# Matmuls by segment, modulation units summed by DVE and a float32r ones matmul, and Q's raw slabs in h's context columns, in a two-layer GLA and attention trunk

## The reference

```python
mod_x = jnp.einsum('bd,lde->lbe', jax.nn.silu(c), w_ada) + b_ada[:, None, :]
mod_c = jnp.einsum('d,lde->le', jax.nn.silu(c_ctx), w_ada) + b_ada
for i in range(DEPTH):                       # DEPTH = 2
    sh1, sc1, g1, sh2, sc2, g2 = jnp.split(mod_x[i][:, None, :], 6, axis=-1)
    ...                                      # the same of mod_c for the context
    hx = rmsnorm(x, norm_mix[i]) * (1.0 + sc1) + sh1
    hc = rmsnorm(ctx, norm_mix[i]) * (1.0 + csc1) + csh1
    ...                                      # layer 0: gated linear attention (GLA), both directions
    ...                                      # layer 1: windowed attention with sinks; q, k rotated (RoPE)
    x = x + g1 * ox
    x = x + g2 * swiglu(rmsnorm(x, norm_ffn[i]) * (1.0 + sc2) + sh2, ffn_w_in[i], ffn_w_out[i])
    if not last:                             # the context goes through layer 0 alone
        ctx = ctx + cg1 * oc
        ctx = ctx + cg2 * swiglu(...)
return rmsnorm(x, norm_final)
```

## Time and profile before

| | us |
|---|---|
| median of 3 runs | 1669.13 |
| the profiled execution, its own time | 1669.12 |
| its span from first to last instruction | 1667.4 |
| PE busy in the span | 1618.1 |
| DVE busy in the span | 864.4 |
| ACT busy in the span | 577.4 |
| mean granted clock of TensorE, as a share | 0.989 |

### The profile page before, as it was taken

One profiled execution on the slowest core, in us unless ns is written; L12 is line 12 of the kernel. 1 busy time (PEld: TensorE's weight loads), 2 busy tenths in 40 slices (PEclk: granted clock), 3 DMA queues, 4 the chain that ended last, 5 costly groups with the idle time before them and its releaser, 6 DMA issues.

```text
span 1667.4 us, 24130 instructions
## 1 busy us (share of the span) xinstructions
PE 1618.1 (97%) x9568; PEld 1370.2 (82%) x9568; DVE 864.4 (52%) x1426; ACT 577.4 (35%) x833; POOL 99.2 (6%) x96
## 2 busy tenths in 40 slices
PE   7999999999999999999999999979999999999998
PEld 5889988888888888888888888757778788888886
DVE  5314436644576566556566336678755533333334
ACT  4315447542432111122102124457744422222223
POOL 0000000000000000000000000036540000000003
PEclk8999999999999999999999999979999999999999
DMA  9341310013443433343343213320003232333332
GB/s 335 100 128 54 106 44 26 26 51 102 127 127 101 125 127 112 115 126 102 125 126 103 74 57 108 101 76 2 1 1 101 76 101 87 90 100 101 101 88 88
DMA packets 197310, 156.07 MB, mean 94 GB/s; under 512 B 6691, under 2 KB 194255, under 8 KB 197231
## 3 DMA queue, kind: packets, MB, share of 16 engines
q1 hardware_dynamic: 197230, 154.97, 30.4%
HBM read 149.71 MB, written 2.10 MB: 91 GB/s over the span
## 4 chain that ended last, share of the span: by engine, by line
PE 88%; DVE 4%; ACT 4%; issue 1%; SPq 1%; DMA 1%; DVEq 0%; ACTq 0%
PE ps L577 85%; PE ps L1110 1%; ACT w_hi L1189 1%; DVE w_lo L1667 1%; DMA ada_pre<-in_w_ada 1%; PE ps L1115 1%; SPq L376 1%; DVE q_st L2192 1%; DVE h_lo L1730 1%; DVE scaled L1721 0%; ACT h_hi L1239 0%; ACT pr L1624 0%; DMA q_sw<-q_rot 0%; PE ps L892 0%; SPq L495 0%
## 5 line engine op out<-in xcount | busy, mean ns | idle before, releaser
L577 PE MATMUL ps<-h_hi,w_hi 128*128 128x256 f32 (+1 forms) x1392 | 422.3, 362 | 6.9 <-DVE w_lo L1667 6.8
L577 PE MATMUL ps<-h_hi,w_lo 128*128 128x256 f32 (+1 forms) x1392 | 413.6, 355 | 0.0
L577 PE MATMUL ps<-h_lo,w_hi 128*128 128x256 f32 (+1 forms) x1392 | 410.1, 353 | 0.0
L1667 DVE TENSOR_TENSOR w_lo<-w_raw,w_hi 128x2048 fp32r<-128x2048 f32 (+1 forms) x88 | 197.2, 2240 | 219.1 <-ACT w_hi L1189 218.9
L577 PEld LDWEIGHTS ps<-h_hi,w_hi 128*128 128x128 f32 x1392 | 257.3, 190 | 51.9 <-issue 13.5
L1189 ACT ACTIVATE w_hi<-w_raw 128x2048 fp32r<-128x2048 f32 (+1 forms) x88 | 165.1, 1876 | 386.0 <-DMA w_raw<-in_ffn_w_in 207.3
L577 PEld LDWEIGHTS ps<-h_lo,w_hi 128*128 128x128 f32 x1392 | 263.7, 189 | 38.3
L577 PEld LDWEIGHTS ps<-h_hi,w_lo 128*128 128x128 f32 x1392 | 262.9, 189 | 37.0
L577 PE MATMUL ps<-a_hi,w_hi 128*128 128x512 f32 (+1 forms) x528 | 160.5, 359 | 0.0
L577 PE MATMUL ps<-a_hi,w_lo 128*128 128x512 f32 (+1 forms) x528 | 160.1, 358 | 0.0
L577 PE MATMUL ps<-a_lo,w_hi 128*128 128x512 f32 (+1 forms) x528 | 158.0, 354 | 0.0
(11 more groups left out here) (246 smaller groups left out, 2011.7 us busy)
## 6 DMA issues: line engine op xcount, KB each, us to landing
w_raw<-in_ffn_w_in SPq DMA_DIRECT2D x88, 512.0 KB, 4.9
ada_w<-in_w_ada SPq DMA_DIRECT2D x41, 1024.0 KB, 5.3
w_raw<-in_ffn_w_out SPq DMA_DIRECT2D x32, 512.0 KB, 4.4
w_raw<-in_gla_w_in SPq DMA_DIRECT2D x24, 512.0 KB, 4.9
ada_pre<-in_w_ada SPq DMA_DIRECT2D x7, 1024.0 KB, 11.8
w_raw<-in_ffn_w_out SPq DMA_DIRECT2D x16, 384.0 KB, 3.5
w_raw<-in_gla_w_o SPq DMA_DIRECT2D x8, 512.0 KB, 7.2
w_raw<-in_swa_w_o SPq DMA_DIRECT2D x8, 512.0 KB, 5.0
```

What stands on the lines that cost most here:

```text
L577: return pe.matmul(o, w, r, start=start, stop=stop, skip_group_check=skip)
L1667: dve.tensor_tensor(w_lo[s][:, 0:kc, :], raw_of(n)[:, 0:kc, :], w_hi[s][:, 0:kc, :].bitcast(F32), ALU.subtract).then_inc(wlo_ok, 1)
```

## The change

1. **Order within a chunk.** Wherever PE works on both segments, the loops become segment (LAT first), ch, product: six matmuls of 512 columns, then six of 256.
2. **Units 0 to 3 and 12 to 39** go by DVE's `unit_acc`. ACT makes a float32r copy of the result (`unit_high`), DVE the rest (`unit_low`), and PE sums both with two float32r matmuls of 512 columns against a matrix of ones, which leaves the sums in all partitions of bank 7. DVE picks the diagonal: a product with `ident`, a reduction, and the bias (`store_sum`). Units 4 to 11 stay with `unit`. There are two sets of `u_acc`, `u_hi`, `u_lo` and ones, one for units 0 to 3 and one for the rest.
3. **Places.** In the GLA's Q and K the sums stand ahead of chunks 1 and 7 of slab 2 and chunk 6 of slab 3; unit 3's in V0 at tile 2, where the first gate pre-activation moves to tile 3. FFN0's first two slabs have no unit any more, and all others up to slab 45 have one (28 in all). SP asks for unit 1 ahead of slab 3.
4. **Q's stage.** Raw slabs Q0 + 2 and Q0 + 3 land in the context columns of `h_hi` and `h_lo` (`raw_c`), free once the KV slab is done. SP asks for them before the first swap. ACT splits Q0 + 1 between chunks 4 and 5 of h, and Q0 + 2 ahead of `raw_q(0)`; DVE's split of Q0 + 2 comes before K's low part. `q_rot` sets rotate over four, `v_tok` is copied by ACT, and `high(5)` comes before `raw_q(6)`.

The core of the diff:

```diff
-                    for ch in chunks:
-                        blk = slice(ch * P, (ch + 1) * P)
-                        for j, (w, r) in enumerate(((w_hi, x_hi), (w_hi, x_lo), (w_lo, x_hi))):
-                            for sg in segs:
+                    for sg in reversed(segs):
+                        for ch in chunks:
+                            blk = slice(ch * P, (ch + 1) * P)
+                            for j, (w, r) in enumerate(((w_hi, x_hi), (w_hi, x_lo), (w_lo, x_hi))):
...
         def unit_sum(a, i=0):
             pe.wait_ge(mod_ok, a + 1 + i)
-            pe.wait_ge(ada_done, a + 1 + i)
-            for e in range(2):
-                for m in range(2):
-                    last = mm(bank(6, 2 * e + m, 1), u_acc[:, m, e * P:(e + 1) * P], ones[:, 0:1], True, True)
+            pe.wait_ge(ul_ok, sum_no(a) + 1 + i)
+            for j, u in enumerate((u_hi, u_lo)):
+                last = mm(bank(7), ones_r[u_set(a)][:, :], u[u_set(a)][:, :, :].rearrange("p m n -> p (m n)"), j == 0, j == 1)
             last.then_inc(turned, 1)
...
-        unit(0)
-        slab(QK0 + 2, 0, h_in, BOTH, turns=0, before={5: lambda: unit(1), 7: lambda: unit_turn(1)})
-        unit(2)
-        slab(QK0 + 3, 0, h_in, BOTH, turns=2)
-        unit(3)
+        pe.wait_ge(or_ok, 1)
+        slab(QK0 + 2, 0, h_in, BOTH, before={1: lambda: unit_sum(0), 7: lambda: unit_sum(1)})
+        slab(QK0 + 3, 0, h_in, BOTH, before={6: lambda: unit_sum(2)})
         pe.wait_ge(gwl_ok, 1)
-        pe.wait_ge(row_ok, V0)
+        pe.wait_ge(mod_ok, V0)
...
-                    first_slab(n, 2 * l, segs, turn=unit_of(n) - 1 if has_unit(n) else None)
-                    a = unit_of(F0)
-                    slab(n + 1, 0, h_in, segs, k_wait=h_wait(2 * l + 1, per),
-                         before={1: lambda: unit_turn(a), 4: lambda: unit(a + 1), 7: lambda: unit_turn(a + 1)}
-                         if has_unit(n) else {})
+                    first_slab(n, 2 * l, segs, turn=U1 - 1 if l == 0 else None)
+                    slab(n + 1, 0, h_in, segs, k_wait=h_wait(2 * l + 1, per))
...
+        def unit_high(a, i=0):
+            act.wait_ge(ada_done, a + 1 + i)
+            act.wait_ge(turned, a + 1 + i)
+            if a == 0:
+                act.wait_ge(wlo_ok, QK0 + 3)
+            act.activation(u_hi[u_set(a)][:, :, :], u_acc[u_set(a)][:, :, :], ACT.Copy).then_inc(row_ok, 1)
...
+        def unit_low(a, i=0):
+            dve.wait_ge(row_ok, a + 1 + i)
+            dve.tensor_tensor(u_lo[u_set(a)][:, :, :], u_acc[u_set(a)][:, :, :], u_hi[u_set(a)][:, :, :].bitcast(F32),
+                              ALU.subtract).then_inc(ul_ok, 1)
+
+        def store_sum(a, i=0):
+            dve.wait_ge(turned, a + 2 + i)
+            part = u_acc[u_set(a)][:, :, :].rearrange("p m (e n) -> p (m e) n", n=P)
+            dve.tensor_tensor(part, bank(7).rearrange("p (c n) -> p c n", n=P),
+                              ident[:, :].rearrange("p (o n) -> p o n", o=1).to_broadcast([P, 4, P]), ALU.mult)\
+               .then_inc(up_ok, 1)
+            dve.wait_ge(up_ok, 2 * sum_no(a) + 1 + i * 2)
+            dve.tensor_reduce(den[:, :], part, AX.X, ALU.add).then_inc(up_ok, 1)
...
+            dve.tensor_tensor(mods[:, bass.ds(e, 2), :], den[:, :].rearrange("p (m e) -> p e m", m=2),
+                              v3(vec[:, bass.ds(V_BADA + e, 2)], 2), ALU.add).then_inc(mod_ok, 1)
...
                 if ahead:
                     split(n + 1, i, kc)
                 if a_ is not None:
-                    store_unit(a_, i * 2)
+                    unit_low(a_, i * 2)
+                    store_sum(a_, i * 2)
...
         load_slab(Q0, 0, cols(swa_w_qkv[0], 0))
-        load_slab(Q0 + 1, 0, cols(swa_w_qkv[0], 256))
+        for n in range(Q0 + 1, SO0):
+            load_slab(n, 0, cols(swa_w_qkv[0], (n - Q0) * 256))
...
-        modulate(2, KV_EDGE, (LAT,), 48, 2, 8)
+        modulate(2, KV_EDGE, (LAT,), 48, 2, 5)
+        act.wait_ge(slab_done, KV0 + 1)
+        split(Q0 + 1)
+        modulate(2, KV_EDGE, (LAT,), 48, 5, 8)
...
+        act.wait_ge(slab_done, Q0 + 1)
+        split(Q0 + 2)
         raw_q(0)
+        act.wait_ge(yr_ok, 1)
+        for g in range(2):
+            last = act.activation(k_st[64 * g:64 * g + 64, 0, g, :], y_rot[64 * g:64 * g + 64, :], ACT.Copy)
+        last.then_inc(qh_ok, 1)
         raw_q(1)
-        split(Q0 + 2)
+        act.wait_ge(vt_done, 1)
+        act.activation(v_tok[:, :, :].rearrange("p t n -> p (t n)"), S67, ACT.Copy).then_inc(vt_ok, 1)
```

More of the change, by code:

```diff
@@ L87, in trunk @@
     x_in = at("x_in", H, [P, TILES, D])
+    raw_c = [at(f"raw_c{j}", H + j * DC * ROW, [P, DC, T]) for j in range(2)]
     so_hi = at("so_hi", H, [P, DC, LX], F32R)
@@ L695, in step @@
             pe.wait_ge(h_ok, 2 * k + 2)
[L696 to L699, removed]
+            for sg in (LAT, CTX):
+                for ch in range(2):
+                    blk = slice(ch * P, (ch + 1) * P)
+                    for j, (w, x_) in enumerate(((w_hi, h_hi), (w_hi, h_lo), (w_lo, h_hi))):
                         last = mm(seg(b0, ch, sg), w[s][:, k, blk], x_[:, k, sg[0]:sg[1]], start=(k == 0 and j == 0 and
@@ L796, in first_slab @@
                     last.then_inc(bw_done, 1)
-                    if turn is not None:
-                        unit(turn + 1)
                 pe.wait_ge(rl_ok, 8 * e + k + 1)
[L800 to L803, removed]
+                for sg in reversed(segs):
+                    for ch in range(2):
+                        blk = slice(ch * P, (ch + 1) * P)
+                        for j, (w, r) in enumerate(((w_hi, raw_hi), (w_hi, raw_lo), (w_lo, raw_hi))):
                             last = mm(seg(b0, ch, sg), w[s][:, k, blk], r(e, k, sg), start=(k == 0 and j == 0 and
@@ L844, in _ @@
             for t in range(TILES):
-                if t == 1:
-                    if n == V0:
-                        pe.wait_ge(gl_ok, 1)
+                if t == 1 and n > V0:
                     unit_turn(n - 1)
-                if t == 2:
+                if t == 2 and n == V0:
+                    pe.wait_ge(gl_ok, 1)
+                    unit_sum(n - 1)
+                if t == 2 + int(n == V0):
                     pe.wait_ge(mod_ok, n + 1)
@@ L1312, in _ @@
         split(QK0 + 4)
+        unit_high(2)
         qk_out(QK0 + 3)
-        unit_row(3)
+        unit_high(3)
         act.wait_ge(gl_done, 1)
@@ L1469, in first, with up @@
                 act.activation(a_hi[:, 0, a:T], tmp[2 + s][:, a:T], ACT.Copy).then_inc(ah_ok, 1)
-            def up(n, i, u, fu, kc, ahead=True):
+            def up(n, i, u, fu, kc, ahead=True, a_=None):
                 if ahead:
                     split(n + 1, i, kc)
+                if a_ is not None:
+                    unit_high(a_, i * 2)
                 s = n % 2
@@ L1531, in _ @@
         last.then_inc(vb_ok, 1)
-        split(Q0 + 1)
-        act.wait_ge(yr_ok, 1)
-        for g in range(2):
-            last = act.activation(k_st[64 * g:64 * g + 64, 0, g, :], y_rot[64 * g:64 * g + 64, :], ACT.Copy)
-        last.then_inc(qh_ok, 1)
         def raw_q(f):
@@ L1573, in _ @@
         high(4)
+        high(5)
         raw_q(6)
-        high(5)
         high(6)
@@ L1880, in _ @@
         dve.memset(g_w[:, :, :], 0.0).then_inc(gw_ok, 1)
+        dve.tensor_copy(ones_r[0][:, :], ones[:, :]).then_inc(or_ok, 1)
+        unit_acc(0)
         split(QK0 + 2)
-        store_unit(0)
+        unit_low(0)
+        store_sum(0)
+        unit_acc(1)
         split(QK0 + 3)
-        store_unit(1)
-        store_unit(2)
+        unit_low(1)
+        store_sum(1)
+        unit_acc(2)
         split(QK0 + 4)
+        unit_low(2)
         dve.wait_ge(gwh_ok, 1)
@@ L1889, in _ @@
            .then_inc(gwl_ok, 1)
-        store_unit(3)
+        store_sum(2)
+        unit_acc(3)
+        unit_low(3)
+        store_sum(3)
         def logs(h, d):
@@ L2124, in ffn @@
                             if has_unit(n):
-                                store_unit(unit_of(n) + e, i * 2)
+                                unit_low(unit_of(n) + e, i * 2)
+                                store_sum(unit_of(n) + e, i * 2)
                             residual(n + e, i, segs, l * 48 + 40, i * 4 + 2 * e, None)
```

110 lines of the change are left out of this document (62 added, 48 removed).

## The result

The change takes the kernel from 1670.08 us (median of 4 runs, 1669.12 to 1673.90) to **1647.59 us** (4 runs, 1646.06 to 1648.03): a ratio of 0.9859, 95% interval 0.9842 to 0.9877. Forecast was 1638.9, range 1631 to 1651. The profiled execution took 1647.26 us, its span 1645.5; before it was 1667.4. So 21.9 us of the 30.2 in the sum are in the traces, and 8.3 are missing.

What follows compares the result with a forecast made beforehand. The prediction took PE, busy 97% of the span, as the bound. Gains of 9.5 + 10.5 + 5.8 + 1.4 + 3 = 30.2 us, taken from 1669.1, gave 1638.9 us, range 1631 to 1651.

Steps and rivals of the forecast that it cites:

- Part 1: Mixed slabs' matmuls by segment: 0.038 us less in each of 248 FFN0 chunks, 9.5 us gained.
- The 139 us: Estimated cost of ordering by segment if the skill's rule on weight loads held for 256-column matmuls; left out of the sum.
- Part 2: FFN0's modulation units: two float32r matmuls per sum in place of four fp32 ones, 10.5 us gained.
- Rival D: FFN0: unit_acc, unit_high, unit_low and PE's sum become a ring per slab, making the kernel slower, 1692 us; chance 0.04.
- Part 3: Units 0 to 3, up to the gate projection: three sums replace four units and three turns, 5.8 us gained.
- Part 4: FFN0's first two slabs: two units and two turns leave, 1.4 us gained, 1.9 becomes a wait for w_lo.
- Part 5: Q's slabs: split waits go, attention's table load comes sooner behind the swap, rotation, high, raw_q chain; 3 us gained.
- rival B: Q's stage gains all that PE's waits promise, as swaps land sooner: 5 us more, with early end 1633.5; chance 0.12.
- Rival A: Ordering by segment brings nothing and FFN0's slow pattern stays: 1648 us; chance 0.12.

Runs made afterwards that it cites:

- e5: The changed kernel with the order of the 512- and 256-column segments turned round in every second chunk; 1643.30 us.
- e6: The changed kernel with each whole FFN0 slab split by width, all chunks of 512 columns and then all of 256; 1642.23 us.
- e2: The kernel before with only the matmuls of mixed slabs ordered by segment; 1666.48 us, ratio 0.9973.
- e10: The kernel before with only the DVE-summed units, float32r sums and unit moves; alternating widths and Q's stage as before; 1655.22 us.
- e4: The changed kernel with attention started before the last two head pairs are rotated, those rotations spread over attention's first passes; 1643.55 us.
- e3: The kernel before with only Q's stage changed: late raw slabs into h's context columns, splits ahead, new ACT and DVE order; 1666.96 us.
- e7: The kernel of e1 without FFN0's 28 unit sums on PE, so its result is not the reference's; 1637.43 us (two runs).
- e8: The kernel of e1 with each FFN0 sum written as 256, 512, 256, 512 columns, the last a dummy; 1651.76 us (two runs).
- e1: The changed kernel with its mixed slabs back in the old order of alternating 512 and 256 columns; 1650.61 us.

## Why the prediction was right in its direction and 8 us short

**Part 1, the step that failed.** "The new chunk is thus 6 x 0.227 + 6 x 0.120 = 2.082." Both durations came from long runs of one width, and I took them for runs of six. e5 and e6 show that the first matmuls after a change from 256 to 512 columns are slower: 0.018 us a chunk with one such change in each. The count of 248 slow chunks was off too: before, the slow pace begins with FFN0's first sum at 491.50, and the seven chunks ahead of it in slab 18 ran at 2.08:

```profile
484.91 0.51 PE L577 MATMUL ps<-h_hi,w_lo 128*128 128x256 f32 x2
...
485.95 0.51 PE L577 MATMUL ps<-h_hi,w_lo 128*128 128x256 f32 x2
```

So FFN0 gave 241 x 0.020 - 7 x 0.020 = 4.7 us, not 9.5. The sentence beside it, "nothing gained where alternation takes 2.08 already", hid a loss: 2.100 or 2.120 against 2.08 in the QK and GO slabs, some 0.5 us in QK (e2's gate projection comes that much later) and 0.6 in GO. Together 5.9 of the 8.3 us. I had named 0 as the lower bound and 9.5 as the upper one, and taken the upper for two rows that did not show the new order's own pattern.

By the chunk's own rows the Trainium skill's rule that was weighed in the prediction (TensorE: Matmul & The Clock Gate, "What overlaps and what doesn't") does not show here either: 256-column matmuls of the new order come 0.118 apart, with a weight load for each. The 139 us worked out beside that rule do not follow from it, though: PEld counts as many loads as PE matmuls in the old order too (x3585 and x3586 in FFN0, rows 3), so that by the rule both orders would pay the same.

**Part 2, right.** 26 x 0.89 - 28 x 0.46 = 10.3, forecast 10.5. e10 has the slab distance of 17.41 and the 10.3 us by itself. Rival D, the ring, did not come: the cover was 1.6 us as worked out.

**Part 3, right to half a microsecond.** 5.3 for 5.8, and the half is Part 1's: QK's slabs at 2.120 and 2.100 and not 2.08 (with alternating widths, in e10, the gain is 5.9). The chain worked out for DVE held: PE never waited for a sum there. PE's row after:

```profile
110.88 0.40 PE L593 MATMUL ps<-h_hi,g_whi 128*128 128x512 f32 x1
```

The gate projection was forecast at 110.4.

**Part 4, right but for 0.4.** PE's row of slab 18:

```profile
472.84 0.49 PE L593 MATMUL ps<-h_hi,w_hi 128*128 128x512 f32 x1 [1.09 <-DVE w_lo L1697]
```

1.0 for 1.4. The wait for w_lo sets the start, so the gain hangs on when w_lo comes, and DVE's split begins at 470.41 and not 473.71: counted from GO's end 0.2 us earlier than before, where I had worked out 0.5. That is the step that was off here. The wait is 1.1 and not 1.9, since PE, at 2.100 to 2.120 a chunk, comes later to it; that changes nothing of the gain.

**Part 5, right.** 3.4 to 3.9 for 3. The chain of swap, rotation, high and raw_q did hold attention's start, and rival B (PE's end sets it) is refuted by the wait of 9.9. e4 adds what I had not asked: whether that chain has to be there at all.

**GO's clock.** 1.6 us of the gap are a fall of the clock that before's profiled execution lacked; a term that no step of mine had, and none that the change brings (e3).

**What closes the sum.** 30.2 - 4.8 (Part 1 in FFN0) - 1.1 (Part 1 elsewhere) - 1.6 (GO's clock) + 0.4 (Part 5) - 0.4 (Part 4) = 22.7, against 21.9. Of the last 0.8, 0.2 is in Part 2 and 0.4 behind attention; 0.2 I don't trace. The 0.4 is a draw of the one execution: from the start of PE's last matmul to the end of the span the trace after has 8.7 us and all eleven others 7.7, a loss of 1.0, and 0.6 were won between attention and there. Rival A (segments bring nothing, 1648) gave nearly the measured time, but not for its reason: the segments do bring something (e2, 4.5 us), and about as much was lost where it was not looked for (GO's clock, that tail, Part 1's chunks outside FFN0). That 1647.59 lies in the stated range is no merit of Part 1: the range reached down to its lower bound.

## What to carry to other kernels

A duration read in a long run of one shape is the price of the middle of that run. Before it is multiplied by hundreds, look for a stretch of the trace with the new order's own pattern, or take the change of shape as a term with bounds; and when matmuls of two widths can't be one run each, make the runs as long as the waits allow (e6: about 5 us for a loop turned inside out). An engine's long wait at the head of a stage is worth one question, which of the results it waits for the first instruction really uses (e4: 4.0 us). And one profiled execution is one draw: a stage in which the clock differs between two traces is checked against a third before it is put down to the change.

## What the runs showed of the hardware

- Runs of float32r matmuls with 128 x 128 weights: 512 columns every 0.227 us and 256 columns every 0.120 in the middle of a run; the first six of 512 columns behind a run of 256 take 1.39 us and not 1.36, the first six of 256 behind 512 take 0.71 and not 0.72. From the sixth on the 512-column ones are at 0.227 (e5, e6).
- Strict alternation of 512 and 256 columns has more than one steady pace: 2.080 or 2.120 us for twelve. It keeps one for hundreds of matmuls, and takes another at a break as small as 20 ns (e7) or at nearly each of 28 sums in turn (e8). The order by segment has two as well, 2.100 (all of FFN0 from slab 18 on) and 2.120 (56.8 to 78.0 us, GO's first slab); what picks one is not shown.
- A sum over partitions as two float32r matmuls of 512 columns against ones costs PE 0.46 us; as four fp32 matmuls with one column it cost 0.89. DVE pays for it: 0.7 us for u_lo and 1.6 for the diagonal's product, reduction and addition, all in idle time here.
- Near the start of GO PE's clock falls to the lower level, at a price of 1.6 us, in nine of twelve traces; in the other three it doesn't, with PE as busy ahead of it (19.6 of 22 us, after and before). A fall of the same price in the second feed-forward network (before) cost nothing in the end, since without it (after) PE waits 1.0 us for h_lo and 0.3 longer for w_lo right behind that place. Kernels with the same code in that stage stand on both sides (e1 against e7 and e8).
